# Expert steps of two 32-row groups on four column tiles, two row buffers, one packed table entry a step, 8 KB weight pieces

## The reference

```python
t = h.reshape(B * S, D)                       # 512 x 1024, after rmsnorm
g_idx = jnp.argmax(t @ w_rg + b_rg)           # 1 of 4 groups of experts
top_v, top_i = lax.top_k(le_sel, 2)           # 2 of the 4 experts in that group
hid = silu(t @ w_gate[e]) * (t @ w_up[e])     # 16 experts: 1024 -> 512
out = out + (hid * combine) @ w_down[e]       # 512 -> 1024
```

## Time and profile before

| | us |
|---|---|
| three runs | 659.71, 660.79, 662.58 |
| median | 660.79 |
| the profiled execution | 661.52 |
| its span, first to last instruction | 659.7 |
| PE busy | 614.5 (93%) |
| ACT busy, DVE busy, POOL busy | 202.3, 215.6, 59.8 |
| HBM read, written | 142.66 MB, 10.23 MB |

### The profile page before, as it was taken

The page is one execution under the profiler, slowest core; times in us unless marked ns, Lnnn a source line. Parts: engine busy times, 40 slices in busy tenths (PEclk is TensorE's granted clock), DMA queues, the critical chain, the costliest instruction groups (busy, mean ns, idle before and its releaser), DMA issues.

```text
span 659.7 us, 9372 instructions
## 1 busy us (share of the span) xinstructions
PE 614.5 (93%) x3378; PEld 389.2 (59%) x3379; DVE 215.6 (33%) x480; ACT 202.3 (31%) x440; POOL 59.8 (9%) x105
## 2 busy tenths in 40 slices
PE   6999999999999999996899999999999999935995
PEld 6998877879989899953233333333333333314883
DVE  3521265456253442365011110111111011165663
ACT  5532354545444533342110100101010010152674
POOL 0000000000000000002112212121221212110000
PEclk8999999999999999978899999999999999986998
DMA  8743114111111079854989999998998999955001
GB/s 311 210 153 128 64 65 128 64 65 65 65 65 65 1 262 393 311 224 155 330 322 398 398 394 397 382 343 294 395 397 326 379 399 396 406 217 204 32 33 64
DMA packets 76416, 153.34 MB, mean 232 GB/s; under 512 B 7960, under 2 KB 27296, under 8 KB 76128
## 3 DMA queue, kind: packets, MB, share of 16 engines
q1 hardware_dynamic: 72144, 139.77, 57.8%
q0 software_dynamic: 3952, 12.85, 5.1%
q10 hardware_dynamic: 288, 0.28, 0.2%
HBM read 142.66 MB, written 10.23 MB: 232 GB/s over the span
## 4 chain that ended last, share of the span: by engine, by line
PE 85%; DVE 5%; DMA 4%; ACT 2%; SPq 2%; issue 2%; DVEq 0%; POOLq 0%; POOL 0%; ACTq 0%
PE bank L1556 22%; PE bank L1296 13%; PE bank L1297 12%; PE bank L1298 12%; PE bank L1580 11%; PE bank L1378 2%; DMA ring_gu<-in_w_up 2%; PE bank L1503 2%; PE bank L1544 2%; SPq L577 2%; PE bank L1351 2%; DVE ple_lo L1229 2%; DMA gmix<-in_norm_mix 1%; PE bank L1568 1%; PE bank L1392 1%
## 5 line engine op out<-in xcount | busy, mean ns | idle before, releaser
L1556 PE MATMUL bank<-ring_gu,rowsT 128*64 128x512 f32 x736 | 165.2, 601 | 2.8 <-issue 1.7
L1556 PEld LDWEIGHTS bank<-ring_gu,rowsT 128*64 128x64 f32 x736 | 51.0, 138 | 100.8 <-issue 99.6
L1580 PE MATMUL bank<-ring_dn,hidT 128*64 128x512 f32 x368 | 84.0, 598 | 1.4 <-DVE hidT L1200 1.4
L865 ACT ACTIVATE silu_g<-bank 128x256 f32<-128x256 f32 x23 | 8.8, 383 | 236.5 <-PE bank L1556 236.5
L1045 DVE TENSOR_TENSOR w_lo<-w_raw,w_hi 128x2048 fp32r<-128x2048 f32 x18 | 41.3, 2292 | 76.8 <-ACT w_hi L730 69.6
L1195 DVE TENSOR_TENSOR hid<-silu_g,bank 128x256 f32<-128x256 f32 x23 | 9.7, 421 | 166.0 <-ACT silu_g L865 166.0
L1296 PE MATMUL bank<-w_hi,hT_hi 128*128 128x256 f32 x192 | 56.1, 292 | 0.8 <-issue 0.8
L1297 PE MATMUL bank<-w_lo,hT_hi 128*128 128x256 f32 x192 | 54.9, 286 | 0.0
L1298 PE MATMUL bank<-w_hi,hT_lo 128*128 128x256 f32 x192 | 54.8, 286 | 0.0
L1296 PE MATMUL bank<-hT_hi,w_hi 128*128 128x512 f32 x128 | 50.8, 397 | 0.0
L1580 PEld LDWEIGHTS bank<-ring_dn,hidT 128*64 128x64 f32 x368 | 24.4, 136 | 44.7 <-issue 44.7
(11 more groups left out here) (210 smaller groups left out, 906.5 us busy)
## 6 DMA issues: line engine op xcount, KB each, us to landing
ring_gu<-in_w_gate SPq DMA_DIRECT2D x32, 1024.0 KB, 14.4
ring_gu<-in_w_up SPq DMA_DIRECT2D x32, 1024.0 KB, 15.3
ring_dn<-in_w_down SPq DMA_DIRECT2D x16, 2048.0 KB, 14.0
w_raw<-in_w_in SPq DMA_DIRECT2D x14, 1024.0 KB, 5.0
w_raw<-in_w_out SPq DMA_DIRECT2D x4, 1024.0 KB, 4.8
ple_gate_raw<-in_w_ple_gate SPq DMA_DIRECT2D x1, 4096.0 KB, 26.3
yg<-y_rows SPq DMA_DIRECT2D x8, 512.0 KB, 7.5
xr<-in_x SPq DMA_DIRECT2D x4, 512.0 KB, 9.2
```

Source lines behind the costliest of these rows:

```text
L1556: last = T.matmul(b_gu[q * BLK:(q + 1) * BLK, :], rowsT[:, k % 4, k // 4, :], ring_gu[s][:, k, :, q * UC:(q + 1) * UC], start=(k == 0), st ...
L1580: last = T.matmul(b_dn[q * BLK:(q + 1) * BLK, :], hidT[:, kf % 2, kf // 2, :], ring_dn[s][:, kf, q * (D // 2):(q + 1) * (D // 2)], start=( ...
```

## The change

- Experts' pairs are cut into groups of `GRP` = 32 rows; a step takes two successive groups, which may be of two experts. `total` and `cum_i` count steps (half of the groups, rounded up).
- In gate_up and down four matmuls take the place of two, each with 32 columns of weights, on four column tiles: two groups by two halves of the columns. Each has the 512 moving columns that it had. When the two groups are of one expert, both read the same weights.
- `ROW_BUFS` is 2: POOL issues gather(b+1) where it issued gather(b+3), and one gather less ahead of the loop.
- PE reads one packed entry a step (`blk_code`: slot pair and two load counts) and takes it apart in registers; the branch goes to one of six copies of the products. PE's loop isn't unrolled by three; a branch on the parity of the turn picks the row buffer.
- Weight pieces: K is dealt to partitions so that each partition's piece is 8 KB in one run of HBM, for gate, up and down; `ring_gu` is laid out to match, and the transposes read with a step (`rows[buf][:, j::4]`, `hid[:, j::2]`).
- Two spare rows of `h2_rows` are filled by a small DMA, and unused places gather from them.
- The routing's tables are larger: 16 x 16 comparisons for 16 x 8, 50 groups for 32 blocks, four more operations for the packed entry.

The core of the diff:

```diff
 BLK = 64
-BPE = SEQ // BLK
-
-MAX_BLOCKS = (TOP_K * SEQ - N_EXPERTS) // BLK + N_EXPERTS
-ROW_BUFS = 3
+GRP = 32
+ROW_BUFS = 2
+
+LOADS_0 = 8
+LOADS_1 = 64
+GPE = SEQ // GRP
 GROUP = 6
-PE_GROUP = 3
-TABLE = MAX_BLOCKS + ROW_BUFS
+
+MAX_GROUPS = (TOP_K * SEQ - N_EXPERTS) // GRP + N_EXPERTS
+MAX_BLOCKS = GROUP * (-(-(MAX_GROUPS // 2) // GROUP)) + 1
+TABLE = MAX_BLOCKS + 3
...
-        ring_gu = [at(f"ring_gu{i}", RING_AT[i], [P, KD, 2, D_EXPERT]) for i in range(RING)]
+        ring_gu = [at(f"ring_gu{i}", RING_AT[i], [P, 2, KD, D_EXPERT]) for i in range(RING)]
...
-                    src = w[bass.ds(e, 1)].rearrange("o (k p) f -> p (o k) f", p=P)
-                    sp.dma_start(ring_gu[slot][:, ks, n, :], src[:, ks, :]).then_inc(s_gu[slot][half], 16)
+                    src = w[bass.ds(e, 1)].rearrange("o (q p j) f -> p (o q) j f", p=P, q=2)
+                    sp.dma_start(ring_gu[slot][:, n, ks, :], src[:, half]).then_inc(s_gu[slot][half], 16)
...
+            sp.dma_start(h2_rows[2 * SEQ:2 * SEQ + 2].rearrange("r (a c) -> (r a) c", c=BLK),
+                         small_tab[BLK:BLK + 2 * HALF // BLK, 0:BLK]).then_inc(s_h2, 16)
...
-            def gather(b, buf, n_columns):
-
-                rows_of = column(src_now[buf], src_row, b)
+            def gather(b, buf, now, n_columns):
+
+                rows_of = column(src_now[now], src_row, b)
...
             for b in range(ROW_BUFS):
-                gather(b, b, b + 1)
-
-            pool.wait_ge(xT_done, 1)
-            gather(ROW_BUFS, 0, ROW_BUFS + 1)
+                gather(b, b, b, b + 1)
 
             def step(b, k, turn):
 
-                pool.wait_ge(xT_done, b + 1)
-                gather(b + ROW_BUFS, (1 + k) % ROW_BUFS, 2 * b + ROW_BUFS)
-                scatter(b - 1, k % 2, 2 * b + (ROW_BUFS + 1))
+                pool.wait_ge(xT_done, b)
+                gather(b + 1, k % ROW_BUFS, (2 + k) % 3, 2 * b + 1)
+                scatter(b - 1, k % 2, 2 * b + 2)
...
+                n_grp = 2 * MAX_BLOCKS
+                link(V.tensor_tensor(grp_ge[:], iota_blk[0:1, 0:n_grp].unsqueeze(2).to_broadcast([1, n_grp, 16]),
+                                     cum[0:1, :].unsqueeze(1).to_broadcast([1, n_grp, 16]), ALU.is_ge))
+                link(V.tensor_reduce(grp_e[:], grp_ge[:], X, ALU.add))
...
-            def in_slot(b, products):
-
-                loads = pe.value_load(blk_loads[0:1, bass.ds(b, 1)], min_val=1, max_val=6)
-                slot = pe.value_load(blk_slot[0:1, bass.ds(b, 1)], min_val=0, max_val=RING - 1)
-                with pe.If(slot < 1):
-                    products(0, loads)
+            def in_slots(b, products):
+
+                code = pe.value_load(blk_code[0:1, bass.ds(b, 1)], min_val=LOADS_0 + LOADS_1, max_val=8 * LOADS_1 - 1)
+                pair, loads = code % LOADS_0, [code // LOADS_0 % (LOADS_1 // LOADS_0), code // LOADS_1]
+                with pe.If(pair < RING):
+                    with pe.If(pair < 1):
+                        products((0, 0), loads)
+                    with pe.Else():
+                        with pe.If(pair < 2):
+                            products((1, 1), loads)
+                        with pe.Else():
+                            products((2, 2), loads)
...
                 pe.wait_ge(s_rows[buf], 16 * loads)
                 for j in range(4):
-                    last = T.transpose(b_xT[:, j * P:(j + 1) * P], rows[buf][:, j * P:(j + 1) * P], ident)
+                    last = T.transpose(b_xT[:, j * P:(j + 1) * P], rows[buf][:, j::4], ident)
                 last.then_inc(xT_done, 1)
...
-                        for q in range(2):
-                            last = T.matmul(b_gu[q * BLK:(q + 1) * BLK, :], rowsT[:, k % 4, k // 4, :],
-                                            ring_gu[s][:, k, :, q * UC:(q + 1) * UC],
-                                            start=(k == 0), stop=(k == KD - 1))
+                            pe.wait_ge(s_gu[slots[0]][k // (KD // 2)], 32 * loads[0])
+                            if slots[1] != slots[0]:
+                                pe.wait_ge(s_gu[slots[1]][k // (KD // 2)], 32 * loads[1])
+                        for g in range(2):
+                            for q in range(2):
+                                o = g * BLK + q * GRP
+                                last = T.matmul(b_gu[o:o + GRP, :], rowsT[:, k % 4, g, k // 4, :],
+                                                ring_gu[slots[g]][:, :, k, q * UC:(q + 1) * UC],
+                                                start=(k == 0), stop=(k == KD - 1))
...
             def step(b, k, turn):
                 hidden_transpose(b - 1)
                 gate_up(b)
-                rows_transpose(b + 1, (2 + k) % ROW_BUFS, PE_GROUP // ROW_BUFS * turn + ((2 + k) // ROW_BUFS + 1))
+                with pe.If(turn % ROW_BUFS < 1):
+                    rows_transpose(0, turn // ROW_BUFS + 2)
+                with pe.Else():
+                    rows_transpose(1, turn // ROW_BUFS + 2)
                 down(b - 1)
 
-            over_blocks(pe, total, step, group=PE_GROUP)
+            over_blocks(pe, total, step, group=1)
```

More of the change, by code:

```diff
@@ L70 @@
 MASKED = -1e30
+ROUND = 1.5 * 2.0 ** 23
 RING = 3
@@ L231, in trunk @@
         p_sb = at("p_sb", 16, [P, NT, D_PLE])
-        rows = [at(f"rows{i}", kb, [P, D // 2]) for i, kb in enumerate((64, 66, 99.25))]
-        rowsT = at("rowsT", 68, [P, 4, 2, BLK])
+        rows = [at(f"rows{i}", 64 + 2 * i, [P, D // 2]) for i in range(ROW_BUFS)]
+        rowsT = at("rowsT", 68, [P, 4, 2, 2, GRP])
         silu_g = at("silu_g", 70, [P, UC])
         hid = at("hid", 71, [P, UC])
-        hidT = at("hidT", 72, [P, 2, 2, BLK])
+        hidT = at("hidT", 72, [P, 2, 2, 2, GRP])
         y_blk = [at(f"y_blk{i}", kb, [P, D // 2]) for i, kb in enumerate((73, 76, 101.25))]
@@ L296, in trunk @@
         dst_row = tiny("dst_row", [P, TABLE], I32)
-        src_now = [tiny(f"src_now{i}", [P, 1], I32) for i in range(ROW_BUFS)]
+        src_now = [tiny(f"src_now{i}", [P, 1], I32) for i in range(3)]
         dst_now = [tiny(f"dst_now{i}", [P, 1], I32) for i in range(3)]
         cum_i = tiny("cum_i", [1, N_EXPERTS + 1], I32)
-        blk_slot = tiny("blk_slot", [1, 32], I32)
-        blk_loads = tiny("blk_loads", [1, 32], I32)
+        blk_code = tiny("blk_code", [1, MAX_BLOCKS], I32)
         dqT = at("dqT", 124, [P, HEADS, SEQ])
@@ L386, in trunk @@
         rows_f = at("rows_f", 102, [P, 2 * TABLE])
[L387 to L393, removed]
+        grp_ge = at("grp_ge", 40, [1, 2 * MAX_BLOCKS, 16])
+        grp_e = at("grp_e", 46, [1, 2 * MAX_BLOCKS])
+        grp_rge = at("grp_rge", 43.25, [1, 2 * MAX_BLOCKS, 5])
+        grp_q = at("grp_q", 46.25, [1, 2 * MAX_BLOCKS])
+        code = [at(f"code{i}", 46.5 + 0.125 * i, [1, MAX_BLOCKS]) for i in range(3)]
+        steps_f = at("steps_f", 45.75, [1, N_EXPERTS])
+        steps_r = at("steps_r", 45.875, [1, N_EXPERTS])
+        h2_rows = nc.dram_tensor("h2_rows", [2 * SEQ + 2, HALF], F32, kind="Internal").ap()
         y_rows = nc.dram_tensor("y_rows", [2 * N_PAIRS + 2, HALF], F32, kind="Internal").ap()
@@ L991, in route @@
                 link(V.tensor_tensor(first[:], cum[:], nb1[:], ALU.subtract))
-                link(V.tensor_scalar(first64[:], first[:], float(BLK), None, ALU.mult))
+                link(V.tensor_scalar(first32[:], first[:], float(GRP), None, ALU.mult))
                 link(V.tensor_tensor(slots[:], b_rank[:, 0:NT * 16].rearrange("p (t e) -> p t e", t=NT),
-                                     first64[:].unsqueeze(1).to_broadcast([P, NT, 16]), ALU.add))
+                                     first32[:].unsqueeze(1).to_broadcast([P, NT, 16]), ALU.add))
                 for k in range(TOP_K):
@@ L1276, in _ @@
             for buf in range(ROW_BUFS):
-                dve.wait_ge(s_rows[buf], 16 * ((total + (2 * ROW_BUFS - 1 - buf)) // ROW_BUFS))
+                dve.wait_ge(s_rows[buf], 16 * ((total + ROW_BUFS - buf) // ROW_BUFS))
             stage6_a(0)
@@ L1561, in products @@
                     last.then_inc(gu_done, 1)
-                in_slot(b, products)
+                in_slots(b, products)
             def hidden_transpose(b):
```

118 lines of the change are left out of this document (65 added, 53 removed).

## The result

| | us |
|---|---|
| after, four runs | 748.30 to 757.36, median 755.61 |
| before, four runs on the same chip | 659.71 to 663.18, median 661.68 |
| ratio | 1.140, 95% interval 1.132 to 1.148 |
| the profiled execution of after, its span | 757.36, 755.4 |

The change makes the kernel 94 us slower. The forecast was 703 us, in a range of 664 to 745: the sign was right, the size less than half of it.

What follows compares the result with a forecast made beforehand. TensorE bound the kernel, transfers close behind; after the change the gather loop would set the period. 660.8 us plus 31.1 (loop), 12 (clock) and 0.3 (table), less 0.7 (tail), gave 703 us, range 664 to 745.

Steps and rivals of the forecast that it cites:

- Gather: On POOL, gather(b+1) stands behind scatter(b-2), issued 4.06 us after down's end, setting a period of 16.0 or 13.3 us.
- Which step meets which: Steps 4, 8, 12, 19 and most of 17 gather on idle queues; 13 steps at 16.0 us, 5 at 13.3.
- Landing: Gathered rows take 6.2 us to land under weight loads, 3.55 us with idle DMA engines; 8 KB pieces add 0.
- Clock: Gaps on PE around the row transposes lower TensorE's clock in one in four loaded steps: +12 us, range 0 to 47.
- Behind the wait: On PE, from the rows' landing to the down product: 2.1 us, between 0.59 and 2.7, covering the strided transposes.
- Rival (a): PE's sequencer works ahead of the row wait, 0.59 us from landing to down product; 665 us, chance 12%.
- Four tiles: In the products, four column tiles run side by side as two do: gate/up stays 7.0 us, down 3.6 us.
- (c): In the products, four column tiles go in pairs, a step takes 22.2 us; 817 us, chance 7%.
- (e): In the products, four tiles share less well than two, a down product takes 4.5 us; 719 us, chance 8%.
- Rest: Routing table work on DVE +0.3 us, SP's extra DRAM copy 0, earlier gate matrix at the end -0.7 us.
- Start: Start of the expert stage: no term of its own; the copies counted only as one more level of branches.
- Rival (b): Gathers land in time, within 3.3 us of issue: 626 us, or 657 us at a 3.55 us landing; chance 10%.

Runs made afterwards that it cites:

- small pieces: The changed kernel with the 2 and 4 KB weight pieces and plain transposes of the kernel before: 745.26 us, ratio 1.125.
- the gather ahead: The changed kernel, two row buffers kept, with POOL issuing gather(b+2) instead of gather(b+1) in step b: 661.01 us, ratio 0.998.

## Why the forecast was right in kind and wrong in size

Between the +42.7 us of the forecast and the 95.7 between the spans lie 53 us. The steps that failed are three terms of the sum: the landing (+18.7) and the clock (+18.7), both put too low, and the start of the stage (+16.7), put at nothing. The mechanism of the loop was right.

*Gather.* Right. "What decides" was the place of the gather behind scatter and y. Down's end to the gather's issue: 4.10 us, forecast 4.06. A step on idle queues: 13.3 us, forecast 13.3. Which step meets which was right but for 17: steps 4, 8, 12 and 19 are idle; 17 was counted with them, but lands in 4.85 us and loses clock. It belongs to the loaded, which makes 14.

*Landing.* Wrong by size. The forecast took 6.2 us, the median of the earlier trace rows, for a loaded queue. That median belongs to gathers whose place among the weights' transfers was that of before, where nobody waited for them, and it is a median where a sum needs the mean: 6.45 us for the gathers of its steps 3 to 22. With the order alone changed, loaded landings are 6.93 us; the 8 KB pieces, taken at 0 with 0.9 us as the other end, added 0.64. Together 117.0 us of landing in 18 steps where 98.4 were forecast: +18.7.

*Clock.* Wrong by size: the rows at hand bounded it between never and each loaded step, and one in four was taken, 12 us. It was each of the 14, by 1.4 to 2.95 us, 30.7 us in all: +18.7. Where it was lost it cost 2.2 us on average, not the 3.6 of a whole down product; it was the number of times that failed. A period that repeats puts nearly the same two gaps ahead of the same product every time, and in after that meant every time. It need not: with the gap filled it was four of 14.

*Behind the wait.* Landing to down product: 34.2 us in 18 steps, 1.9 each, forecast 2.1: -3.6. Rival (a), 0.59 us, is refuted. The strided transposes add nothing there, as forecast: with plain ones (small pieces) it is 1.9 as well. Where nothing covers them, as in the kernel before, they cost 0.15 us a step.

*Four tiles.* Right: 64 records in 7.07 us, 0.11 us each, a quarter of the untiled 0.43 of the earlier trace rows. Rivals (c) and (e) are refuted. The 2.38x for three column tiles that the forecast cited from the Trainium skill (TensorE: Matmul & The Clock Gate, Measured speedup vs the span model) does not carry over to these: four fp32 tiles run at 3.9x.

These terms give 18.7 + 18.7 - 3.6, and 1.4 from 3.64 and 4.10 where 3.6 and 4.06 stood: 35 us, which is what the loop (321.2) took over 286.5 (274.5 and 12). A loaded period is 19.1 us, forecast 16.0 and 0.9 of clock.

*Rest.* The table and the tail came to +1.1 us, forecast -0.4.

*Start.* Missed altogether: 16.7 us. The six copies were costed as "one more level of branches". The price that it knew was that of a branch to code at hand; the second, for the first arrival at code not yet fetched, rows of before do not show, since its three copies are a quarter of the code and no branch there takes over 0.35 us. The Trainium skill (Advanced Engine Details and Errata, Control Flow Timing) has a compare-and-branch at about 108 ns; in the kernels with six copies the long ones took 2.5 to 6.8 us. The same page (ISA Cache) describes instruction memory in lines of 16 KB, 256 instructions each; the 16 KB pieces here agree. A copy of gate/up is 128 instructions of TensorE by the trace's records, six are 768; by that page's figure this is an estimated three lines, where the 192 instructions of before are less than one. The length of the jump is not all of it: the fourth long branch, 2.90 us, passes only four row transposes.

*Rival (b)*, gathers in time, gave 626 us. It did not happen, but the gather ahead makes it so, and then the time is 661, and 638.8 without the long branches, with 10.9 us of it spent on weights: the weights' stream would have bound before 626 was reached.

What stays open: the branch of 5.83 us holds two fetches, which last 1.0 us each in the records; what fills the rest isn't known, nor why in the other long branches the fetch begins 0.2 to 2.3 us after the branch does. Whether another layout of the copies inside the loop would hide them was not tried.

## What to carry to other kernels

When a transfer is moved behind work that depends on its own consumer, cost the loop that closes, not the wait: its period is the sum of all its parts, and every part that was hidden (a landing under load, the lowered clock behind a gap, branches held up by a wait) is now counted in each turn. Take a landing time from steps in which the transfer stands where it will stand, as a mean, and let the range hold a clock loss in every turn of a repeating pattern. Before adding copies of a loop body, count the instructions that the first pass must get past.

## What was not expected of the hardware

- The first pass through a loop with six copies of its products has branches that stop TensorE's queue for 2.5 to 6.8 us; later passes through the same loop show none over 0.3 us. Fewer copies shorten it (at most 1.97 us with three).
- Idle matmuls that fill a gap of 4 us make the run faster: 739.45 against 755.61 us, clock 0.955 against 0.904.
- Transposes that read SBUF with a step cost 0.15 us for six of them when they stand bare.
